# A gather's place in SBUF: eleven dead rows join the places, and the choice among them goes by expected release

## The chip, the core and the metric

The kernel runs on one core of a Trainium2 chip. The metric is the device time of one execution in microseconds (us); the time of a kernel is the median of its runs.

## What is computed

One layer of an encoder trunk over 512 tokens of width 1024, all in fp32. The first part (adaLN, a combined projection, eight heads of neighbourhood attention and four of differential attention, output projection, post-LN) takes roughly the first 315 us of the span, with its last pieces spread over what follows. The change concerns the second part, PEER retrieval, for each chunk of 128 tokens:

```python
qc = (xc @ w_query).reshape(PEER_CHUNK, PEER_HEADS, 2, PEER_DKEY // 2)
...
expert = jnp.take_along_axis(cand_i, best_j, axis=-1)     # 16 experts per token and head, 8 heads
g = jax.nn.softmax(best_s, axis=-1)
u_e = expert_down[expert]                                 # one row of 1024 floats per expert
act = jax.nn.gelu(jnp.einsum('chkd,cd->chk', u_e, xc), approximate=False)
v_e = expert_up[expert]
return jnp.einsum('chk,chkd->cd', (g * act).astype(xc.dtype), v_e)
```

With 4 chunks, 8 heads and 16 experts this is 512 sets. A set is one expert of one head for 128 tokens: it needs 128 rows of `expert_down` and 128 rows of `expert_up`, each of 4 KB, each set of rows 512 KB.

## The kernel before, in words

Tokens lie on the 128 partitions. The sets are numbered `at` = 0 to 511 in the order of `HEAD_AT`; one step through this order is called a slot below. Each set has two gathers, an indirect DMA each, of 128 rows of 4 KB into a **place**: 128 partitions by 1024 floats of SBUF.

- A **down** gather is read by VectorE at L1528: one fused product and sum with the tokens, `dots[:, at]`, then `dot_done` goes up by one. Four dots make a quarter: ScalarE takes the GELU (L993), VectorE multiplies by the gate (L1483, `weigh`), ScalarE builds four diagonal matrices `diag[:, j]` (L1163). There are 16 diagonals; that of set `at` may be built once `up_done` has reached `at - 15`.
- An **up** gather is read by TensorE at L939: two matmuls `diag[:, j]` times the place, added into a PSUM pair; each appears in the trace as two instructions, so four for a set. Then `up_done` goes up by one.

TensorE also works off `STEPS`, pieces of the remaining projections, one or more behind each up: `query` (L753), `key_scores` (L787), `ln2_row` (L735), transposes (L761). ScalarE empties their banks at L1032 at a fixed point of its own order, six slots after the group's end (`EVAC_AFTER`), and waits there for `pe_group`, which TensorE raises at the end of each group. The query groups of the later tiles lie in slots 178 to 209, 222 to 289 and 326 to 357.

GpSimd issues the gathers (L681) in the fixed order `GATHERS`: down 0, down 1, ..., and from down 7 on each down is followed by the up that lies 7 slots back, so downs and ups alternate. Before each gather stands one wait, `wait_for_place`: the place's last holder must have been read (`dot_done` or `up_done`). Which place a gather gets is fixed when the program is built. `place_for` gives the first 8 gathers places 0 to 7; a place that becomes free later is taken the first time the count of downs reaches its slot; otherwise the gather takes the place whose last holder was issued longest ago. So with k places in use each one returns k gathers later, be its holder a down or an up.

Places come in as memory dies: 8 from the start, 12 from slot 61, 16 from slot 269, 20 from slot 305 (`LATE_PLACES`, each a weight slot of four rows, released by a query group and opened `PLACE_SETS` = 16 slots later). VectorE's own order around the places: `add_mix` of the last output tile at slot 90 (`ADD_AT`), LayerNorm steps at slots 168 to 175 (`LN_FROM`), `residual(0)` and `residual(1)` after heads 12 and 16, a copy of the tokens into PSUM before every fourth head (`u_copied`).

## Time and profile before

| | us |
|---|---|
| median of 3 runs | 1824.02 |
| lowest and highest | 1817.2, 1826.44 |
| profiled execution, its own time | 1825.07 |
| its span | 1823.3 |
| first gather issued | 316.6 |
| last gather issued | 1796.4 |

The profiled execution is one of the same kind as the timed ones; 1.8 us lie around its span. The hardware profiler gives each instruction of each engine with its start and duration, each DMA packet, and the clock granted to TensorE. A wait is named by what ended it. "remote" stands there where the semaphore's update arrived and no instruction of this core that ends shortly before it can be found as its sender; "issue" where nothing of the kind ended it. The gather of one place is 0.5 MB; the share of a DMA window is the mean busy share of 16 DMA engines, GB/s what all queues moved together.

### The profile page before, as it was taken

How to read it: one execution, taken by the hardware profiler on the slowest of the kernel's cores; microseconds unless marked ns; L12 is line 12 of the kernel's file. 1: busy time of each engine (PE TensorE's matmuls, PEld its weight loads, DVE VectorE, ACT ScalarE, POOL GpSimd, SP SyncE). 2: the span in 40 equal slices, each digit the busy share in tenths (PEclk: the TensorE clock that was granted, in tenths of full speed). 3: DMA queues.
4: the chain of work that ended last, by engine and by line, in shares of the span. 5: the costliest groups of instructions: out<-in, count | busy, mean ns of one | idle time of the engine just before them, and what ended most of it. 6: DMA issues, size and time to landing. Idle time of an engine off the chain costs nothing.

```text
span 1823.3 us, 14455 instructions
## 1 busy us (share of the span) xinstructions
PE 1473.1 (81%) x4072; PEld 684.6 (38%) x4072; DVE 1116.8 (61%) x2733; ACT 438.7 (24%) x1119; POOL 983.7 (54%) x1054
## 2 busy tenths in 40 slices
PE   6999988888988897766987988876787776776775
PEld 4444557534433553222432333422343322222222
DVE  5550367776666766676565667656455674577644
ACT  3111345322221322122222222212122121122111
POOL 1000000666666666666566666666676666667663
PEclk9999999999999999998899999999898999899999
DMA  9965402999999999999899999999999999999996
GB/s 308 380 236 112 162 4 46 338 366 356 371 355 392 407 373 366 368 366 364 310 359 409 378 366 376 373 358 373 376 360 357 374 361 383 372 348 374 374 378 244
DMA packets 190617, 604.97 MB, mean 332 GB/s; under 512 B 30897, under 2 KB 31305, under 8 KB 190379
## 3 DMA queue, kind: packets, MB, share of 16 engines
q0 software_dynamic: 147456, 536.94, 77.6%
q1 hardware_dynamic: 42027, 64.30, 10.5%
q10 hardware_dynamic: 1056, 2.82, 0.5%
q8 instruction: 34, 0.56, 0.1%
q14 instruction: 44, 0.36, 0.1%
HBM read 600.64 MB, written 3.34 MB: 331 GB/s over the span
## 4 chain that ended last, share of the span: by engine, by line
PE 34%; POOL 19%; issue 14%; DMA 13%; DVE 11%; another core or an unknown queue 6%; ACT 1%; SPq 1%; DVEq 0%; POOLq 0%; ACTq 0%
PE pair L939 17%; POOL big L681 14%; PE pair L691 9%; POOL region_v L681 5%; DMA big<-in_expert_up,expert_idx 5%; DMA region_v<-in_expert_up,expert_idx 3%; DVE big L1528 3%; PE pair L753 3%; DMA big<-in_expert_down,expert_idx 2%; DMA region_v<-in_expert_down,expert_idx 2%; PE pair L779 1%; DVE region_v L1528 1%; PE pair L718 1%; SPq L519 1%
## 5 line engine op out<-in xcount | busy, mean ns | idle before, releaser
L939 PE MATMUL pair<-big 128*128 128x512 f32 x1460 | 728.7, 625 | 196.7 <-DMA big<-in_expert_up,expert_idx 93.3
L1528 DVE CUSTOM_DVE_ANT_0 big<-big,pair 128x1024 f32<-128x1024 f32 x363 | 441.2, 1219 | 267.0 <-DMA big<-in_expert_down,expert_idx 176.6
L939 PEld LDWEIGHTS pair<-big 128*128 128x128 f32 x1460 | 267.2, 196 | 576.2 <-issue 550.7
L681 POOL DMA_INDIRECT big<-in_expert_up,expert_idx x365 | 346.2, 949 | 247.7 <-remote 106.8
L681 POOL DMA_INDIRECT big<-in_expert_down,expert_idx x363 | 346.4, 954 | 123.6 <-issue 101.7
L939 PE MATMUL pair<-region_v,big 128*128 128x512 f32 x588 | 296.1, 625 | 78.9 <-DMA region_v<-in_expert_up,expert_idx 35.9
L1528 DVE CUSTOM_DVE_ANT_0 region_v<-region_v,pair 128x1024 f32<-128x1024 f32 x149 | 181.6, 1219 | 109.9 <-DMA region_v<-in_expert_down,expert_idx 75.2
L1163 ACT ACTIVATE big<-ident,big 128x128 f32<-128x128 f32 x512 | 163.5, 390 | 354.6 <-issue 185.4
L939 PEld LDWEIGHTS pair<-region_v,big 128*128 128x128 f32 x588 | 106.5, 196 | 228.2 <-issue 216.7
L681 POOL DMA_INDIRECT region_v<-in_expert_up,expert_idx x147 | 139.3, 947 | 95.4 <-issue 36.4
L681 POOL DMA_INDIRECT region_v<-in_expert_down,expert_idx x149 | 140.6, 944 | 52.1 <-issue 42.1
L993 ACT ACTIVATE big<-big 128x4 f32<-128x4 f32 x128 | 26.2, 205 | 588.1 <-issue 351.8
L691 PE MATMUL pair<-big 128*128 128x512 f32 (+1 forms) x368 | 151.0, 566 | 0.0
L753 PE MATMUL pair<-big 128*128 128x256 f32 (+1 forms) x640 | 144.3, 343 | 5.8 <-ACT big L1032 3.2
L753 PEld LDWEIGHTS pair<-big 128*128 128x128 f32 x640 | 105.8, 193 | 95.9 <-issue 90.8
L634 POOL TENSOR_SCALAR small<-x_sums 128x4 f32<-128x4 f32 x4 | 0.8, 197 | 257.0 <-ACT big L1043 257.0
L691 PEld LDWEIGHTS pair<-big 128*128 128x128 f32 x368 | 69.1, 192 | 79.9 <-issue 79.6
L1032 ACT ACTIVATE big<-pair 128x512 f32<-128x512 f32 (+2 forms) x74 | 32.9, 454 | 194.8 <-remote 158.0
L779 PE MATMUL pair<-big 128*128 128x512 f32 x128 | 63.4, 594 | 2.5 <-issue 1.6
L1483 DVE SCALAR_TENSOR_TENSOR big<-big 128x4 f32<-128x4 f32 x128 | 28.2, 220 | 48.0 <-ACT big L993 32.2
L1442 DVE CUSTOM_DVE_ANT_1 big<-pair,big 128x256 f32<-128x256 f32 x32 | 12.2, 419 | 60.1 <-PE pair L798 60.0
L993 ACT ACT_TABLE_LOAD x38 | 48.8, 1283 | 0.7
(156 smaller groups left out, 1078.1 us busy)
## 6 DMA issues: line engine op xcount, KB each, us to landing
big<-in_w_ada SPq DMA_DIRECT2D x8, 2048.0 KB, 22.3
big<-in_w_in SPq DMA_DIRECT2D x5, 2048.0 KB, 13.1
big<-in_w_ada SPq DMA_DIRECT2D x16, 512.0 KB, 11.9
big<-in_w_query SPq DMA_DIRECT2D x4, 2048.0 KB
big<-in_expert_up,expert_idx POOLq DMA_INDIRECT x365
big<-in_expert_down,expert_idx POOLq DMA_INDIRECT x363
big<-in_w_out SPq DMA_DIRECT2D x2, 2048.0 KB
big<-na_scr SPq DMA_DIRECT2D x24, 128.0 KB, 4.1
```

What stands on the lines that cost most here:

```text
L519: sp.dma_start(ada_rows[:, k, i, :].rearrange("p (a n) -> p a n", a=2), src[:, :, i, :])\
L681: nc.gpsimd.indirect_dma_start(places[place], None, (expert_down if kind == "down" else expert_up)[0], bass.IndirectOffsetOnAxis(expert_id ...
L691: last = nc.tensor.matmul(ps, a, b, start=(i == 0), stop=(i == len(pairs) - 1))
L718: last = nc.tensor.matmul(bank[b], h_t[:, k, b * P:(b + 1) * P], w_slot[ADA_FIRST][:, k, :], start=(k == 0), stop=(k == KB - 1))
L753: return nc.tensor.matmul(ps[:, 0:n * P], w_slot[query_slot(c, first)][:, k, b * P:(b + 1) * P], src, start=(k == 0), stop=(k == KB - 1))
L779: return nc.tensor.matmul(ps[:, :], src, w_slot[OUT_SLOT[s]][:, k, :], start=(k == 0), stop=(k == KB - 1))
L939: last = nc.tensor.matmul(pair[t % 2][:, s * HALF:(s + 1) * HALF], diag[:, j, :], places[place][:, s * HALF:(s + 1) * HALF], start=(h == 0 ...
L993: nc.scalar.activation(acts[:, head % 2, lo:lo + QUARTER], at_head(dots, head)[:, lo:lo + QUARTER], ACT.Gelu).then_inc(gelu_done, 1)
L1032: nc.scalar.activation(dst, ps, ACT.Copy).then_inc(act_evac, 1)
L1163: nc.scalar.activation(diag[:, j, :], ident[:, :], ACT.Copy, scale=weights[:, head % 2, j:j + 1]).then_inc(diag_done, 1)
L1483: v.scalar_tensor_tensor(out=weights[:, k, lo:lo + QUARTER], in0=gate_exps[:, k, lo:lo + QUARTER], scalar=gate_sum[:, k:k + 1], in1=acts[: ...
L1528: v.tensor_tensor_reduce(out=places[place], in0=places[place], in1=u_cur[:, :], scale=1.0, scalar=0.0, op0=ALU.mult, op1=ALU.add, accum_ou ...
```

## The change

Eleven rows of 4 KB that are dead by a given slot become places 20 to 30: a row of `mods` from slot 102, the `mix_t` region from 104, `u_sb` rows 0, 1 and 2 from slots 142, 206 and 398, the two `ln1_rows` from 188, `x_sb` rows 0 and 1 from 222 and 286, the two halves of `u_t` from 382. Each place's first gather waits for what made the row dead (`first_use`). With more than 12 places in use, an up counts as released `5 * (k - 12) // 4` gathers later than its issue order says (k places in use), so the planner takes a down's place before an up's.

```diff
+EVEN_PLACES, UP_HELD_MORE = 12, 5
+EXTRA_PLACES = [("gate", 102), ("mix", 104), ("u", 142), ("ln1_g", 188), ("ln1_b", 188), ("u", 206), ("x", 222), ("x", 286),
+                ("u_t", 382), ("u_t", 382), ("u", 398)]
...
-ALL_PLACES = PLACES + 4 * len(LATE_PLACES)
+SLOT_PLACES = PLACES + 4 * len(LATE_PLACES)
+ALL_PLACES = SLOT_PLACES + len(EXTRA_PLACES)
...
+OPEN_FROM = [0] * PLACES + [RELEASED_AT[RELEASED_BY[p]] + PLACE_SETS for p in range(PLACES, SLOT_PLACES)] \
+    + [slot for _, slot in EXTRA_PLACES]
...
+def held_until(p):
+
+    last = _held[p][-1]
+    return _order[last] + (UP_HELD_MORE * max(0, sum(map(bool, _held)) - EVEN_PLACES) // 4 if last[0] == "up" else 0)
...
-        if not _held[p] and downs >= RELEASED_AT[RELEASED_BY[p]] + PLACE_SETS:
+        if not _held[p] and downs >= OPEN_FROM[p]:
             return p
-    return min((p for p in range(ALL_PLACES) if _held[p]), key=lambda p: _order[_held[p][-1]])
+    return min((p for p in range(ALL_PLACES) if _held[p]), key=held_until)
...
+        places += [mods[:, 0, :], mix_t.rearrange("p k s -> p (k s)"), u_sb[:, 0, :], ln1_rows[:, 0, :], ln1_rows[:, 1, :],
+                   u_sb[:, 1, :], x_sb[:, 0, :], x_sb[:, 1, :], u_t_rows[:, 0, :], u_t_rows[:, 1, :], u_sb[:, 2, :]]
...
+            def first_use(place):
+
+                extra = place - SLOT_PLACES
+                if PLACES <= place < SLOT_PLACES:
+                    pool.wait_ge(pe_group, INDEX[RELEASED_BY[place]] + 1)
+                elif extra == 0:
+                    pool.wait_ge(dve_evac, EVAC[INDEX[("out", (TILES - 1, 1))]][1])
+                elif extra == 1:
+                    pool.wait_ge(pe_group, INDEX[("out", (TILES - 1, 1))] + 1)
+                elif extra == 2:
+                    pool.wait_ge(u_copied, 3)
+                elif extra in (3, 4):
+                    pool.wait_ge(u_ready, TILES)
+                elif extra == 5:
+                    pool.wait_ge(u_copied, 4)
+                elif extra in (6, 7):
+                    pool.wait_ge(var2_ready, extra - 5)
+                elif extra in (8, 9):
+                    pool.wait_ge(pe_group, INDEX[("query", (3, 3, 2, 2))] + 1)
+                elif extra == 10:
+                    pool.wait_ge(u_copied, 7)
+
             def wait_for_place(gather):
 
                 before = LAST_USE[gather]
                 if before is None:
-                    if PLACE_OF[gather] >= PLACES:
-                        pool.wait_ge(pe_group, INDEX[RELEASED_BY[PLACE_OF[gather]]] + 1)
+                    first_use(PLACE_OF[gather])
                     return
```

The gathers, their order, their number and what reads them stay as they are.

## Rows read from the trace of the kernel before

**Rows 1.** The page: busy time of the engines, and DMA in 40 slices.

```profile
PE 1473.1 (81%) x4072; PEld 684.6 (38%) x4072; DVE 1116.8 (61%) x2733; ACT 438.7 (24%) x1119; POOL 983.7 (54%) x1054
...
DMA  9965402999999999999899999999999999999996
GB/s 308 380 236 112 162 4 46 338 366 356 371 355 392 407 373 366 368 366 364 310 359 409 378 366 376 373 358 373 376 360 357 374 361 383 372 348 374 374 378 244
```

**Rows 2.** Windows by stage: engines' busy us, TensorE clock, DMA share, GB/s.

```profile
345.00:490.00 145.00, 129.31 (x405) 63.49 (x404) 102.12 (x246) 38.14 (x97) 95.77 (x101) 0.99 0.96 356
...
725.00:853.00 128.00, 90.29 (x195) 33.03 (x196) 87.08 (x214) 30.59 (x75) 85.46 (x91) 0.99 0.97 368
...
853.00:881.00 28.00, 20.79 (x33) 8.00 (x32) 11.62 (x22) 9.20 (x20) 12.24 (x14) 0.63 0.75 266
881.00:1097.00 216.00, 181.61 (x468) 82.23 (x466) 140.71 (x351) 45.99 (x123) 141.88 (x151) 0.98 0.99 376
1097.00:1205.00 108.00, 89.86 (x222) 41.14 (x223) 70.12 (x166) 26.30 (x65) 71.48 (x77) 0.97 0.98 372
1205.00:1362.00 157.00, 118.96 (x270) 50.56 (x269) 96.20 (x249) 31.26 (x85) 104.23 (x110) 0.95 0.96 367
1362.00:1795.00 433.00, 315.48 (x655) 121.69 (x653) 266.14 (x648) 88.21 (x237) 285.72 (x302) 0.94 0.97 371
```

**Rows 3.** Timeline of GpSimd at 20 places, two stops.

```profile
1216.14 0.93 POOL L681 DMA_INDIRECT big<-in_expert_down,expert_idx  x1 [0.30 <-issue]
1221.85 0.94 POOL L681 DMA_INDIRECT big<-in_expert_up,expert_idx  x1 [4.77 <-remote]
...
1253.38 0.94 POOL L681 DMA_INDIRECT big<-in_expert_down,expert_idx  x1 [0.30 <-issue]
1258.92 0.94 POOL L681 DMA_INDIRECT big<-in_expert_up,expert_idx  x1 [4.59 <-remote]
```

**Rows 4.** Timeline of TensorE: the matmuls of up 294 and of up 299.

```profile
1199.00 1.95 PE L939 MATMUL pair<-big 128*128 128x512 f32 x4 [1.15 <-DMA big<-in_expert_up,expert_idx]
...
1211.78 1.95 PE L939 MATMUL pair<-big 128*128 128x512 f32 x4 [0.61 <-issue]
```

**Rows 5.** Timeline of GpSimd at 12 places, two stops.

```profile
945.23 0.94 POOL L681 DMA_INDIRECT big<-in_expert_up,expert_idx  x1 [3.62 <-remote]
...
968.37 0.94 POOL L681 DMA_INDIRECT big<-in_expert_up,expert_idx  x1 [2.15 <-remote]
```

**Rows 6.** Windows between two stops and around one (last column GB/s).

```profile
930.00:941.00 11.00, 9.72 (x26) 4.40 (x25) 7.40 (x26) 4.26 (x8) 8.26 (x10) 1.00 1.02 410
941.00:959.00 18.00, 12.74 (x33) 5.60 (x33) 14.28 (x35) 3.23 (x11) 11.23 (x12) 1.00 0.95 344
1237.00:1254.00 17.00, 12.71 (x27) 4.37 (x26) 11.37 (x27) 5.84 (x14) 12.80 (x14) 1.00 1.03 412
1254.00:1273.00 19.00, 11.89 (x25) 4.06 (x24) 12.81 (x36) 1.69 (x6) 11.06 (x13) 1.00 0.89 325
```

**Rows 7.** Waits of GpSimd, 725 to 1795 us: total, times, longest.

```profile
POOL big L681 <- remote: 92.7, 33, 4.8
POOL region_v L681 <- remote: 20.7, 11, 3.9
POOL big L681 <- PE pair L939: 29.2, 25, 5.2
```

**Rows 8.** Timeline of GpSimd, 853 to 881 us: two waits for TensorE.

```profile
868.85 0.94 POOL L681 DMA_INDIRECT region_v<-in_expert_up,expert_idx  x1 [3.45 <-PE pair L939]
...
876.27 0.94 POOL L681 DMA_INDIRECT big<-in_expert_up,expert_idx  x1 [5.24 <-PE pair L939]
```

**Rows 9.** Waits of ScalarE, 725 to 1362 us: total, times, longest.

```profile
ACT big L1032 <- remote: 102.4, 16, 12.0
```

**Rows 10.** Timeline at 1399 us: ScalarE, GpSimd and TensorE after one stop.

```profile
1399.54 0.38 ACT L1032 ACTIVATE big<-pair 128x256 f32<-128x256 f32 x1 [16.62 <-remote]
1399.65 0.94 POOL L681 DMA_INDIRECT big<-in_expert_up,expert_idx  x1 [3.87 <-remote]
...
1400.07 2.05 PE L787 MATMUL pair<-keys_t,big 128*128 128x128 f32 x8 [10.04 <-issue]
```

More of the change, by code:

```diff
@@ L353, in build @@
         v_beside = w_flat[T5_SLOT][:, 3072:4096].rearrange("p (i d) -> p i d", i=2)
+        u_sb = region_h[:, :].rearrange("p (t d) -> p t d", t=TILES)
         places = [w_flat[T5_SLOT][:, i * D:(i + 1) * D] for i in (3, 0, 1, 2)]
@@ L357, in build @@
         places += [w_flat[slot][:, i * D:(i + 1) * D] for slot, _ in LATE_PLACES for i in range(4)]
+        u_t_rows = region_qw[:, 4096:6144].rearrange("p (i d) -> p i d", i=2)
+        places += [mods[:, 0, :], mix_t.rearrange("p k s -> p (k s)"), u_sb[:, 0, :], ln1_rows[:, 0, :], ln1_rows[:, 1, :],
+                   u_sb[:, 1, :], x_sb[:, 0, :], x_sb[:, 1, :], u_t_rows[:, 0, :], u_t_rows[:, 1, :], u_sb[:, 2, :]]
         na_place_sb = mods[0:T5_BUCKETS, 0:2, :].rearrange("p t (e m) -> p (t e) m", m=2 * P)
@@ L360, in build @@
         v_sb = region_v
-        u_sb = region_h[:, :].rearrange("p (t d) -> p t d", t=TILES)
         x_norm = region_v
```

## The prediction, made before the changed kernel was run

> **What bounds the kernel now.** I read the page first, the windows by stage second, the waits and the timeline of GpSimd third, and TensorE's and ScalarE's timelines last. The reader is to see in the page that no engine is full, while DMA stands at nine tenths from the first gather to the last [rows 1]. So the gathers set the end: 1024 of them move 537 MB. But DMA is not evenly full. Between 1237 and 1254 us it moves 412 GB/s, between 930 and 941 us 410; over whole stages it is 356 to 376 [rows 2, 6]. I take 411 as the full rate. What is missing, (1 - rate / 411) times the stage's length, is time: 19.4 us in 345 to 490, then from 725 on 13.4, 9.9, 18.4, 10.2, 16.8 and 42.1 us, in sum 110.8 us [rows 2].
>
> Where is it lost? GpSimd issues one gather every 1.24 us until it stops for 2 to 5 us, again and again: 142.6 us of such waits from 725 on, in the three largest entries [rows 7]. Each stop drains the DMA queues, and the rate is low until they have refilled. Around the stop at 941 us, 344 GB/s over 18 us makes 18 * (1 - 344/410) = 2.9 us lost; around that at 1254 us, 19 * (1 - 325/412) = 4.0 us [rows 6].
>
> What is GpSimd waiting for? At 1221.85 us the gather of up 304 starts. With 20 places its place was last held by the gather 20 earlier, that of up 294. The matmuls of up 294 ran from 1199.00 to 1200.95 [rows 4], over 20 us before GpSimd went on [rows 3]. By 1213.73 even up 299 was through [rows 4]. Either the place was free and something else stopped GpSimd, or TensorE's signal `up_done` arrives late. I take the second, for three reasons. Every long stop stands before an up. Its releaser is TensorE or "remote", an update whose sender had ended long before [rows 7]. And at 1399.5 us ScalarE, which waited 16.62 us for TensorE's `pe_group`, GpSimd (3.87 us) and then TensorE itself (10.04 us) go on within 0.6 us of each other [rows 10]. So while DMA runs full, TensorE's signals are held up, and they come in a bunch once GpSimd has stopped and the queues run down. That is read from this trace; why the chip does it I cannot see.
>
> The length of a run between stops fits. With k places GpSimd can run k/2 ups past the last known `up_done`. At 20 places the stops begin at 1217.07 and 1254.32 us, 37 us or 13 ups apart (up 304, up 317) [rows 3]; at 12 places the gathers after two stops start at 945.23 and 968.37 us, 23 us or 8 ups apart (up 208, up 216) [rows 5]. My estimate is k/2 + 2 ups on average.
>
> **The change part by part.** *The new waits.* Eleven first uses wait for the end of the row's old life. GpSimd issues down 311 at 1216.14 us [rows 3], when TensorE has just done up 299 [rows 4]: 12 slots, of which the order itself makes 7, so the readers are some 5 slots behind. Each opening slot lies at least 12 slots behind its event: 102 against `add_mix` at 90, 188 against LayerNorm's last step at 175, 222 against the residual after head 12 (slot 207), 398 against the copy before head 24 (slot 384). A slot takes 37 us / 13 = 2.85 us, so the 7 slots left over, some 20 us, cover each. The largest consumer delay seen is 16.62 us [rows 10]. I cost them at nothing; without the cover GpSimd would stand with all later gathers behind it, at 1 us per us.
>
> *The places.* A down place and an up place are no longer reused at the same distance. If a down returns after a gathers and an up after a + off, with off = 5 * (k - 12) // 4, and the two alternate, then k = a + off/2. That gives for downs and ups: 13.5 and 16.5 gathers at 15 places (from slot 142), 14 and 20 at 17 (slot 188), 15 and 23 at 19 (222), 16 and 32 at 24 (286), 18 and 38 at 28 (305), 19.5 and 42.5 at 31 (398). Before it was 12, then 16, then 20 for both. So the change gives nearly all the new room to the ups, the ones whose signals are late.
>
> *The stops.* A run of d/2 + 2 ups becomes longer. For the cost of one stop I take 2.9 us at 12 places and 4.0 at 20 [rows 6], 3.4 between, and, above 20, 4.3: a stop cannot lose more than the wait of some 4.7 us [rows 3] with the refill beside it, so the lower bound is 4.0 and the upper one is proportional growth (7 us at d = 42, with which the gain would vanish). I take 4.3 because the longest waits at 20 places are already those of a drained queue.
>
> - 725 to 853 us: runs 8 to 10 ups, cost 2.9 to 3.1: 13.4 us becomes 11.5, gain 1.9.
> - 853 to 881 us: GpSimd waits 3.45 and 5.24 us for ups that TensorE really had not done [rows 8]. With 17 places these waits go; 9.9 us lost falls to the usual 11%, 3.2: gain 6.7.
> - 881 to 1097: runs 8 to 13, cost 2.9 to 3.6: factor 0.76 on 18.4, gain 4.4.
> - 1097 to 1205: runs 10 to 17, cost 3.4 to 4.0: factor 0.69 on 10.2, gain 3.1.
> - 1205 to 1362: runs 12 to 21, cost 4.0 to 4.3: factor 0.62 on 16.8, gain 6.4.
> - 1362 to 1795: runs 12 to 23: factor 0.56 on 42.1, gain 18.5.
>
> The sum is 41.0 us.
>
> *What is late next.* ScalarE also waits for TensorE: for `up_done` at the 16-deep ring of diagonals and for `pe_group` at L1032. When GpSimd stops later, the bunch comes later, and ScalarE, then VectorE (`weigh` needs the GELU), then TensorE stand still for longer. TensorE must catch up from its slack, and each long idle also costs it clock (0.63 in 853 to 881) [rows 2]. The ring lets an up run at most 16 past the last known one, so runs of 21 to 23 are partly cut to some 16 to 19. I take 12 us off for this: a third of the 24.9 us gained behind 1205 us for the ring (8 us), and 4 us for a backlog of two ups of 1.95 us [rows 4] at the end. The net gain is 29 us: 1825.07 - 29 = 1796.1 us for the profiled execution, and 1824.02 - 29 = 1795.0 for the median, which lies 1 us below it.
>
> *Two rules of the skill.* Between stops the row shows 410 to 412 GB/s [rows 6]. The Trainium skill, "DMA: Bandwidth & Descriptors", section "Where 436 GB/s comes from", says that HBM to SBUF is bound at about 358 GB/s per core. By it the gathers already run at the limit and no choice of places could help; the trace does not agree, with 412 against 358. The stop before an up repeats all along GpSimd's row [rows 7]. The Trainium skill, "Perfetto Trace Analysis", section "Optimization Strategy", says that the same gap repeating can mean too little SBUF for the next tile. By it enough places would end all stops; the trace agrees that the stops have to do with places, but not that a longer wait for rows in use is the cause: the row had been read 20 us before.
>
> **The rivals.**
> - *Same loss at any number of places.* For it: the loss is 13% with 8 places, 8.5 to 10.5% with 12, 9.5 with 16, 9.7 to 10.7 with 20 [rows 2]. Longer runs were paid with dearer stops so far. Against it: with a drained queue the cost has a ceiling. If it holds, or if DMA has a limit of its own that the stops only follow, only the real wait of 853 to 881 us goes: 1824.0 - 6.7 = 1817.3 us.
> - *The consumers become the bound (slower).* ScalarE waited 16 times, 102.4 us in all, for `pe_group` between 725 and 1362 us [rows 9]. GpSimd's stop ends these waits today. If up distance no longer stops it, it runs until the downs do, which VectorE leaves unread once ScalarE stands. In these 637 us TensorE is busy 90.3 + 20.8 + 181.6 + 89.9 + 119.0 = 501.6 us [rows 2], so 135 are free, of which 102 go with such waits; 33 are left. The 16 waits may each grow by 33/16 = 2.1 us before TensorE bounds this stretch. Beyond that each us costs 16; the other gains (41 us) are used up from (33 + 41)/16 = 4.6 us on. At 6 us longer: 96 - 33 - 41 = 22 us slower, 1846 us. Against it: a TensorE that is behind slows the gathers through their places, DMA is then not full, and its signals come at once.
> - *All stops vanish.* The full 110.8 us: 1713 us. Against it: GpSimd's issue of 1.24 us per gather hardly leaves DMA behind, so DMA stays full, signals stay late, and each run ends sometime.
>
> **How the numbers follow.** Fewer stops 0.55 (1795; its own range 1778 to 1808), same loss 0.23 (1817), consumers bound 0.17 (1846), no stops 0.05 (1713). Leaving out "no stops" and most of the slow case, the range is 1774 to 1834 us. A measurement of this kernel can tell about 0.5%, 9 us, from no change: 1814.9 and 1833.1. Faster: all of the first and last case and a little of the second, 0.61; same: most of the second and a small part of the third, 0.22; slower 0.17.
>
> **What would show it.** Right: GpSimd's long waits before ups get rarer, some 20 from 725 us on where now some 45 stand, with waits of 4 to 5 us each; behind 1362 us the GB/s rise from 371 to about 387; the waits of 3.45 and 5.24 us are gone; ScalarE's waits at L1032 get longer. Right in places but wrong in sum: stops half as many, GB/s unchanged. Wrong: waits of GpSimd for VectorE at downs, TensorE's busy share over 90% with GpSimd waiting for it, a clock below 0.9 over long stretches. The prediction falls if the late signal is not what GpSimd waits for, or if the price of a stop grows with the length of the run before it.

## The result, and the profile after

| | before | after |
|---|---|---|
| median, us | 1825.23 (4 runs) | 1882.74 (4 runs) |
| lowest and highest | 1817.2, 1826.94 | 1865.01, 1898.14 |
| profiled execution, its span | 1825.07, 1823.3 | 1898.14, 1896.3 |
| TensorE clock over the span | 0.960 | 0.898 |
| last down gather issued | 1796 | 1850 |
| last gather issued | 1803 | 1857 |

The ratio is 1.0287, interval [1.0241, 1.0334]: 52 us slower by the ratio, 57 us between the medians of four, where 29 us faster was forecast, and outside the range. The profiled execution, 1898.14 us, is the slowest of the four and counts as a slow one, so the ratio rests on the other three. What is read from it below also stands, in kind, in the traces of two kernels close to it (e1 and e13 below, executions of 1873.7 and 1870.7 us). The 1796.4 us given for the last gather of the kernel before are those of the last down; five more ups follow it, the last at 1802.6 us.

The page of the changed kernel, the lines that answer to [rows 1]:

```profile
PE 1492.9 (79%) x4072; PEld 717.3 (38%) x4072; DVE 1108.1 (58%) x2733; ACT 437.9 (23%) x1119; POOL 989.1 (52%) x1054
...
PEclk8999999999999999997997988987787888787987
DMA  9975313999999999998999989999877999998983
GB/s 303 360 259 111 120 23 107 343 367 350 369 362 405 402 363 369 374 351 333 369 350 357 372 338 344 362 383 365 314 288 289 361 361 365 354 354 333 353 344 133
```

DMA stands at nine tenths as before, but where [rows 1] has 348 to 383 GB/s in its second half, slices of 288 and 289 stand here, and TensorE's clock falls to seven and eight tenths. Windows by stage, cut where the changed kernel issues the downs of slots 142, 188, 269, 305, 382 and 511, and behind that last down (columns as in [rows 2]):

```profile
728.00:859.00 131.00, 90.71 (x190) 33.42 (x189) 88.09 (x220) 29.86 (x73) 87.83 (x93) 0.94 0.97 370
859.00:1109.00 250.00, 200.60 (x490) 97.20 (x491) 142.86 (x358) 54.56 (x140) 154.05 (x163) 0.88 0.93 351
1109.00:1219.00 110.00, 86.77 (x225) 43.41 (x224) 72.85 (x173) 26.01 (x68) 70.03 (x72) 0.89 0.93 356
1219.00:1463.00 244.00, 173.79 (x381) 77.46 (x381) 126.93 (x333) 44.36 (x118) 146.12 (x154) 0.80 0.86 327
1463.00:1850.00 387.00, 268.71 (x533) 109.13 (x532) 230.28 (x563) 74.80 (x200) 246.99 (x261) 0.84 0.92 354
1850.00:1885.00 35.00, 25.90 (x50) 10.32 (x49) 5.58 (x13) 4.36 (x11) 5.77 (x7) 0.76 0.38 153
```

The same slots took 131.5, 241, 103, 223 and 373 us before, and 15 us lay between the last down's issue and the end of the last up, where now 34 do. So 0.3 us is won up to slot 188; then 9, 7, 21, 15 and 19 us are lost. Up to the last down the clock is 0.80 to 0.94 where [rows 2] shows 0.94 to 0.98 outside of 853 to 881 us. What GpSimd waits for, 728 to 1850 us (total, times, longest), beside [rows 7]:

```profile
POOL big L719 <- DVE big L1566: 89.3, 24, 12.0
...
POOL big L719 <- DVE expert_idx L1359: 24.4, 5, 8.5
POOL big L719 <- PE pair L977: 20.4, 16, 5.2
POOL region_v L719 <- DVE big L1566: 20.2, 9, 5.8
POOL big L719 <- remote: 19.7, 11, 4.3
POOL x_sb L719 <- DVE expert_idx L1359: 11.5, 2, 7.8
```

This is the change of kind. Before, 142.6 us of waits for TensorE or a sender unseen, and 9.8 us for VectorE, none over 0.5. Now 40.1 us of that kind in the two largest entries, and 89.3 + 20.2 + 24.4 + 11.5 = 145.4 us for VectorE: for dots (L1566), whose place a down wants, and for the experts' numbers (L1359). The waits at ups went as forecast; as much came back at downs, and a wait is now up to 12 us long and not 5.

Why is VectorE late? Here is one stop in the timeline: first GpSimd, then VectorE, then ScalarE:

```profile
1381.35 0.94 POOL L719 DMA_INDIRECT big<-in_expert_down,expert_idx  x1 [0.30 <-issue]
1386.54 0.94 POOL L719 DMA_INDIRECT big<-in_expert_up,expert_idx  x1 [4.26 <-remote]
1398.25 0.94 POOL L719 DMA_INDIRECT big<-in_expert_down,expert_idx  x1 [10.77 <-DVE big L1566]
...
1371.70 0.08 DVE L1566 DVE_READ_ACCUMULATOR2_ANT big<- 128x1 f32 x1
1395.44 0.22 DVE L1521 SCALAR_TENSOR_TENSOR big<-big 128x4 f32<-128x4 f32 x1 [23.67 <-ACT big L1031]
...
1368.06 1.28 ACT L1201 ACTIVATE big<-ident,big 128x128 f32<-128x128 f32 x4 [1.89 <-issue]
1391.89 0.38 ACT L1070 ACTIVATE big<-pair 128x256 f32<-128x256 f32 x1 [22.55 <-PE pair L791]
```

VectorE stands 23.67 us for ScalarE's GELU, ScalarE 22.55 us at an evacuation for TensorE. GpSimd goes on gathering until its downs have no place left. And TensorE? Its matmuls in the same time:

```profile
1362.42 1.88 PE L977 MATMUL pair<-big 128*128 128x512 f32 x4
...
1370.17 0.58 PE L791 MATMUL pair<-big 128*128 128x256 f32 x1 [1.48 <-issue]
1372.96 0.59 PE L791 MATMUL pair<-big 128*128 128x256 f32 x1 [2.21 <-issue]
1375.76 1.01 PE L977 MATMUL pair<-x_sb,big 128*128 128x512 f32 x1 [2.21 <-issue]
1377.88 1.01 PE L977 MATMUL pair<-x_sb,big 128*128 128x512 f32 x1 [1.10 <-issue]
1380.66 1.01 PE L977 MATMUL pair<-x_sb,big 128*128 128x512 f32 x1 [1.78 <-issue]
1383.49 1.01 PE L977 MATMUL pair<-x_sb,big 128*128 128x512 f32 x1 [1.81 <-issue]
...
1387.38 3.62 PE L977 MATMUL pair<-big 128*128 128x512 f32 x4
```

and its weight loads:

```profile
1371.57 0.29 PEld L791 LDWEIGHTS pair<-big 128*128 128x128 f32 x1 [2.52 <-issue]
1374.36 0.29 PEld L977 LDWEIGHTS pair<-x_sb,big 128*128 128x128 f32 x1 [2.51 <-issue]
1377.16 0.29 PEld L977 LDWEIGHTS pair<-x_sb,big 128*128 128x128 f32 x1 [2.51 <-issue]
```

A load at 1371.57, a matmul at 1372.96, a load at 1374.36, a matmul at 1375.76: one instruction every 1.4 us, with nothing to wait for ("issue"). Up to 1366 us an up's four matmuls took 1.88 us; from 1366 to 1387 TensorE does little more than one up in 21 us. It began 22 us after GpSimd had gone on from its last stop (1343 us) and ended when GpSimd had stopped again. The granted clock falls only at 1368.4 us, some 3 us after the stretch has begun: the clock follows the gaps here and does not start them. The windows of the full queue, the slow part, and what followed:

```profile
1354.00:1366.00 12.00, 12.00 (x33) 5.91 (x32) 8.72 (x20) 1.79 (x7) 8.90 (x10) 1.00 1.03 413
1366.00:1387.00 21.00, 6.47 (x10) 2.49 (x9) 5.78 (x11) 1.45 (x5) 12.79 (x15) 0.56 1.01 403
1387.00:1399.00 12.00, 12.00 (x27) 6.15 (x27) 3.46 (x15) 4.74 (x10) 1.23 (x2) 0.78 0.15 47
```

The second window has 10 matmuls in 21 us at a granted clock of 0.56, so mostly at the lower level of 1.2 GHz; in the third TensorE catches up while DMA moves 47 GB/s. I call this a slow stretch below, and count it so: a load or matmul of TensorE that waits for no semaphore starts 0.9 to 2.9 us after the one before it, and this happens two or more times with at most 2.9 us between them. The sums are good to some 5 us; a stricter count, without any pair closer than 0.9 us inside, gives 138 us for the changed kernel and 8 for the one before. From slot 142 on the changed kernel has 15 of them, 149 us in sum; the kernel before has 4, 20 us. The clock is at 1.2 GHz for 352 us from slot 142 on, before for 119.

### The profile page after: what moved, and what is told of

It reads as the page before. It is cut to its first block, busy times and chain, and to the rows that moved or that the text cites. A ratio compares the mean times of both kernels' runs of the same rounds, so it can differ in the third digit from the quotient of the medians.

```text
span 1896.3 us, 14455 instructions
## 1 busy us (share of the span) xinstructions
PE 1492.9 (79%) x4072; PEld 717.3 (38%) x4072; DVE 1108.1 (58%) x2733; ACT 437.9 (23%) x1119; POOL 989.1 (52%) x1054
## 4 chain that ended last, share of the span: by engine, by line
PE 32%; DVE 21%; issue 17%; another core or an unknown queue 12%; POOL 7%; DMA 7%; ACT 3%; SPq 0%; DVEq 0%; POOLq 0%; ACTq 0%
PE pair L977 16%; PE pair L729 9%; DVE big L1566 8%; POOL big L719 4%; POOL region_v L719 3%; DMA big<-in_expert_down,expert_idx 2%; DMA big<-in_expert_up,expert_idx 2%; PE pair L791 2%; PE pair L756 2%; PE pair L817 2%; DVE region_v L1566 2%; DMA region_v<-in_expert_down,expert_idx 2%; ACT big L1201 1%; PE pair L836 1%
## 5 line engine op out<-in xcount | busy, mean ns | idle before, releaser
L1566 DVE CUSTOM_DVE_ANT_0 big<-big,pair 128x1024 f32<-128x1024 f32 x360 | 433.5, 1218 | 133.3 <-DMA big<-in_expert_down,expert_idx 58.9
L977 PEld LDWEIGHTS pair<-big 128*128 128x128 f32 x1428 | 281.4, 204 | 559.6 <-issue 490.5
L719 POOL DMA_INDIRECT big<-in_expert_up,expert_idx x357 | 338.0, 947 | 184.3 <-issue 104.6
L977 PE MATMUL pair<-region_v,big 128*128 128x512 f32 x476 | 244.8, 638 | 81.4 <-issue 49.2
L791 PE MATMUL pair<-big 128*128 128x256 f32 (+1 forms) x640 | 149.9, 350 | 37.7 <-issue 35.2
L977 PEld LDWEIGHTS pair<-region_v,big 128*128 128x128 f32 x476 | 92.1, 203 | 196.9 <-issue 178.1
L1566 DVE CUSTOM_DVE_ANT_0 region_v<-region_v,pair 128x1024 f32<-128x1024 f32 x113 | 137.1, 1218 | 43.6 <-DMA region_v<-in_expert_down,expert_idx 32.3
L791 PEld LDWEIGHTS pair<-big 128*128 128x128 f32 x640 | 108.2, 197 | 133.3 <-issue 130.1
L719 POOL DMA_INDIRECT region_v<-in_expert_up,expert_idx x119 | 114.8, 965 | 63.9 <-issue 30.2
L719 POOL DMA_INDIRECT region_v<-in_expert_down,expert_idx x113 | 107.4, 950 | 63.3 <-issue 28.3
L729 PEld LDWEIGHTS pair<-big 128*128 128x128 f32 x368 | 69.1, 192 | 79.9 <-issue 79.6
L977 PE MATMUL pair<-x_sb,big 128*128 128x512 f32 x76 | 41.0, 649 | 10.7 <-issue 10.7
```

Source lines behind the costliest of these rows:

```text
L719: nc.gpsimd.indirect_dma_start(places[place], None, (expert_down if kind == "down" else expert_up)[0], bass.IndirectOffsetOnAxis(expert_id ...
L729: last = nc.tensor.matmul(ps, a, b, start=(i == 0), stop=(i == len(pairs) - 1))
L791: return nc.tensor.matmul(ps[:, 0:n * P], w_slot[query_slot(c, first)][:, k, b * P:(b + 1) * P], src, start=(k == 0), stop=(k == KB - 1))
L977: last = nc.tensor.matmul(pair[t % 2][:, s * HALF:(s + 1) * HALF], diag[:, j, :], places[place][:, s * HALF:(s + 1) * HALF], start=(h == 0 ...
L1566: v.tensor_tensor_reduce(out=places[place], in0=places[place], in1=u_cur[:, :], scale=1.0, scalar=0.0, op0=ALU.mult, op1=ALU.add, accum_ou ...
```

## The experiments

All numbers from slot 142 (some 725 us) on, except time and ratio. A stop is over 1.5 us from the end of one gather's issue to the start of the next. The ratio is to runs of the kernel before on the same chip (its medians there were 1813.2 to 1826.5 us); chips differ, so compare ratios before medians.

| kernel | median us | ratio [interval] | stops (before downs), us | slow stretches, us | at 1.2 GHz, us |
|---|---|---|---|---|---|
| before | 1825.2 | 1 | 45 (2), 147 | 20 | 119 |
| after | 1882.7 | 1.0287 [1.0241, 1.0334] | 43 (24), 199 | 149 | 352 |
| e1 rows alone | 1874.6 | 1.0263 [1.0231, 1.0296] | 36 (26), 186 | 81 | 320 |
| e2 rule alone | 1837.1 | 1.0076 [1.0048, 1.0105] | 42 (13), 150 | 69 | 221 |
| e3 after, up wait as before | 1833.5 | 1.0051 [1.0033, 1.0070] | 44 (2), 160 | 13 | 146 |
| e5 after, up wait at 6 | 1839.1 | 1.0081 [1.0058, 1.0105] | 47 (0), 169 | 0 | 68 |
| e12 after, up wait at 10 | 1832.4 | 1.0039 [1.0024, 1.0054] | 38 (1), 153 | 37 | 208 |
| e6 after, up wait at 14 | 1863.0 | 1.0229 [1.0206, 1.0251] | 47 (25), 173 | 96 | 303 |
| e8 after, ring of 32 | 1871.0 | 1.0283 [1.0247, 1.0320] | 39 (23), 154 | 188 | 336 |
| e13 after, half the signals | 1874.0 | 1.0311 [1.0250, 1.0372] | 38 (22), 170 | 119 | 315 |
| e14 before again | 1814.5 | 0.9998 [0.9981, 1.0014] | 40 (0), 137 | 13 | 142 |
| e15 before, more loads | 1845.4 | 1.0109 [1.0087, 1.0132] | 61 (1), 165 | 92 | 233 |
| e4 before, 2 empty | 1832.7 | 1.0039 [1.0023, 1.0055] | 49 (12), 116 | 13 | 92 |
| e9 before, 5 empty | 1843.1 | 1.0106 [1.0090, 1.0123] | 53 (26), 102 | 0 | 58 |
| e10 before, 8 empty | 1858.0 | 1.0197 [1.0180, 1.0214] | 6 (2), 10 | 0 | 50 |
| e7 before, 16 empty | 1906.4 | 1.0462 [1.0441, 1.0483] | 9 (8), 16 | 0 | 54 |
| e11 after, 8 empty | 1858.7 | 1.0203 [1.0186, 1.0220] | 7 (2), 12 | 0 | 43 |

### The rows, the rule, and a nearer wait

e1 keeps the eleven rows without the rule, e2 the rule without the rows:

```diff
-EVEN_PLACES, UP_HELD_MORE = 12, 5
+EVEN_PLACES, UP_HELD_MORE = 12, 0
```

> The eleven extra places alone, the up rule at zero: every place is reused at the same distance, up to 31 gathers (15.5 ups) instead of 42. Theory A (TensorE's signals arrive late while DMA is full, GpSimd's stop lets them through; an up distance beyond the 16 diagonals moves the stop from GpSimd to ScalarE, VectorE and TensorE): between before and after, 1835 to 1865 us, GpSimd's stops still mostly before ups. Theory B (the new rows themselves, or their first waits, are slow): as slow as after, 1883. Theory C (only the rule for downs, whose distance falls from 20 to 18 or 19, hurts): 1825 or less.

```diff
-EXTRA_PLACES = [("gate", 102), ("mix", 104), ("u", 142), ("ln1_g", 188), ("ln1_b", 188), ("u", 206), ("x", 222), ("x", 286),
...
+EXTRA_PLACES = []
```

> The rule alone, without the extra places: with 20 places downs return after 15 gathers and ups after 25 (12.5 ups). Theory A: slower than before by less than after, 1830 to 1860, since the up distance grows from 10 to 12.5 ups and the down distance shrinks from 10 to 7.5 downs; VectorE's waits for the GELU grow. Theory B: as before, 1825. Theory C: clearly slower, since downs fall from 20 to 15, 1850 or more.

e3 keeps both, with all 31 places, and makes each up wait as near as the kernel before did:

```diff
                 wait_for_place(gather)
+                if kind == "up" and at >= 134:
+                    pool.wait_ge(up_done, at - (6 if at < 262 else 8 if at < 298 else 10) + 1)
```

> The changed kernel with one more wait before each up gather from set 134 on: up_done must have reached what the kernel before needed at that point (6, 8 or 10 ups back). Places, rows, their first waits and both distances stay as changed. Theory A: the stops come back before ups, 20 to 37 us apart, and the time returns to that of before, 1815 to 1835, with TensorE's clock back at 0.95. Theory B and C: as after, 1883.

The rows alone cost 2.6%, the rule alone 0.8%, both 2.9%. For e1 the expectation missed: 1874.6 us lies above its 1835 to 1865, and 26 of 36 stops stand before downs, not ups. Equal distances of 31 gathers are enough for nearly the whole loss, so the rule is not what makes it. e3, with 31 places, is at 0.5%, 9.8 us above the kernel before beside it (1823.7). So the rows and their first waits cost no more than that together; what costs is that GpSimd is no longer stopped early at ups. One of e3's nine executions took 4281.8 us, for a reason not known; the median is hardly moved by it. e3's waits:

```profile
POOL big L721 <- remote: 64.2, 20, 5.6
POOL big L721 <- PE pair L979: 51.9, 31, 6.0
...
POOL region_v L721 <- DVE big L1568: 4.6, 4, 2.0
```

### The distance as a dose

The same line with one distance at all stages: `at - 6 + 1` (e5), `at - 10 + 1` (e12), `at - 14 + 1` (e6).

> The changed kernel, with all 31 places, in which each up gather from up 134 on also waits for TensorE's signal of the up 6 before it (e3_ups_waited: 6, then 8, then 10 before it, 1833.5 us). Theory A (the long run up to the downs is the cost, GpSimd must stop early and at ups): runs of about 8 ups everywhere, few or no stops before downs, ScalarE's and VectorE's long waits gone; time 1815 to 1840 us. If the price of a stop is the same at any length of run, more stops make it slower than e3: 1840 to 1860 us. Rival (the rows or the order of the places themselves cost time): 1870 us and more.

> As e5_near6, but each up gather waits for the signal of the up 14 before it, a distance between that of the kernel before (10) and the longest of the changed kernel (21). Theory A: the time lies between e3_ups_waited (1833.5 us) and the changed kernel (1882.7 us), with some 5 to 20 stops before downs from slot 142 on: 1845 to 1870 us. Rival (the diagonals' ring of 16 alone decides, any wait inside of it is harmless): within 5 us of 1833.5 us. Rival (any stop before a down costs): as the changed kernel, 1875 us and more.

> As e5_near6 (1839.1 us) and e6_far14 (1863.0 us), with the wait at the signal of the up 10 before it at every stage from up 134 on. Theory A as it stands: the price is of two kinds, stops that come oftener when the distance is short (distance 6: 47 stops, none before a down) and stops at downs with ScalarE and VectorE standing still when it is long (14: 25 of 47 before downs). Then 10 lies between or below both: 1820 to 1840 us, at most 10 stops before downs from slot 142 on. If it beats the kernel before (under 1814 us), more rows are worth something once the distance is held at 10. Rival (time grows with the distance from the shortest on): 1848 to 1855 us.

Distances 6, 10, 14 and what the changed kernel has of itself (16 and more) give ratios of 1.0081, 1.0039, 1.0229 and 1.0287; slow stretches 0, 37, 96 and 149 us; 68, 208, 303 and 352 us at 1.2 GHz. With 6 the stops are oftener (47, 169 us), with 14 half of them (25 of 47) stand before downs. The expectations held, but for the stops before downs at 14 (5 to 20 were written, 25 came). The gain over the kernel before that e12 left open did not come: even at the best distance tried, eleven more places are worth nothing. The sum of slow stretches alone doesn't set the time: e15 below has 92 us of them and loses 1.1%, e1 has 81 us and loses 2.6%. In e15 they are some 4 us long each and all stops but one stand before ups; in e1 26 of the 36 stops stand before downs, 147 us of the 186. The windows of e5 from slot 142 to the last down, then of the changed kernel:

```profile
727.00:1813.00 1086.00, 812.06 (x1836) 321.84 (x1836) 673.59 (x1648) 230.35 (x602) 701.53 (x743) 0.98 0.95 362
```

```profile
728.00:1850.00 1122.00, 820.58 (x1816) 360.63 (x1816) 661.01 (x1644) 229.61 (x598) 705.02 (x741) 0.86 0.92 349
```

### The ring of diagonals

e8 gives ScalarE a ring of 32 diagonals from slot 304 on (16 more in two rows of the last late group, so 29 places):

```diff
+        diag_more = w_flat[2][:, 2048:4096].rearrange("p (r m) -> p r m", r=TOPK)
...
-                    if at >= TOPK:
-                        act.wait_ge(up_done, at - TOPK + 1)
+                    if at >= TOPK and not MORE_FROM <= at < MORE_FROM + TOPK:
+                        act.wait_ge(up_done, at - (2 * TOPK if at >= MORE_FROM else TOPK) + 1)
```

> The changed kernel with a ring of 32 diagonals from slot 304 on (two rows of the last late group hold 16 more, so 29 places are left in place of 31). ScalarE then waits for the up 32 before and not for the up 16 before. Theory A with the ring as the main thing that holds ScalarE: faster than the changed kernel by 10 to 30 us, the gain behind slot 304. If ScalarE is held mostly by TensorE's signals of the query and score groups, which it waits for in the same order: within 5 us of 1882.7 us, with ScalarE's waits at that line as long as before.

1871.0 us is 11.7 us less than the changed kernel, but on another chip; the ratio is 1.0283 beside 1.0287, so no gain can be told. Slow stretches grew to 188 us. To let a consumer run further behind TensorE doesn't help while TensorE itself stands. Part of the loss lies at the end: from the last gather's issue to the end of the span it is 38 us in e8 and 40 in the changed kernel, where the kernel before has 21.

### Is it the full DMA queue?

e4, e9, e10 and e7 are the kernel before with 2, 5, 8 and 16 empty instructions of GpSimd ahead of each gather (from some 725 us on in the last three); e11 is the changed kernel with 8. e10's edit, the others' but for the number (e4 has no `if`):

```diff
                 wait_for_place(gather)
+                if n >= 276:
+                    for _ in range(8):
+                        nc.gpsimd.engine_nop()
```

> The kernel before with two empty instructions of GpSimd ahead of each gather, so that it issues a little slower than the 1.24 us it has now. Theory A: if the period comes to 1.29 to 1.35 us, DMA is never quite full between stops, signals come at once, the long stops become rare, and the time is 1024 times the period plus what lies outside: 1740 to 1800 us. If the signals are late for a reason other than full DMA, the period only adds: 1850 to 1900 us, with as many stops as before. If an empty instruction costs under 10 ns, no change.

> The kernel before with 16 empty instructions of GpSimd (some 0.02 us each) ahead of each gather from the 276th on, so that its period grows from 1.243 us to some 1.45 to 1.6 us. It tests whether the signals come late because the DMA queues are full. If so, with a period above the 1.276 us that a gather of 524288 bytes takes at 411 GB/s the queues are never full, the stops of 2 to 5 us before ups go, and the time is set by the period: 748 gathers at 1.45 us are 1085 us for the stretch that takes 1071 us now, so 1825 to 1870 us in all, with fewer than 10 stops. If the lateness has nothing to do with full queues, the stops stay (more than 30) and are added to the longer period: 1900 us and more.

> The kernel before with 5 empty instructions of GpSimd ahead of each gather from the 276th on (e7_paced had 16: period 1.508 us, 9 stops of over 1.5 us). The first two or three fit in the gap that is there anyway, so the period should be some 1.29 us, just above the 1.276 us that a gather takes at 411 GB/s. Theory A (signals are late because DMA runs full; with DMA not full the stops go): 748 gathers at 1.29 us and some 20 us of stops are 985 us for a stretch of 1071 us, so 1740 us; if a queue still fills up now and then, up to 1800 us. Rival (the stops' number only falls at a much slower pace): the longer period comes on top, 1835 us and more.

> As e9_pace5 with 8 empty instructions: period some 1.35 us. Theory A: 748 gathers at 1.35 us and some 16 us of stops are 1026 us in place of 1071 us, so 1780 us. Rival: 1850 us and more.

> The changed kernel (31 places) with the same 8 empty instructions ahead of each gather from the 276th on. Theory A: when the signals are in time, the order of the places no longer matters, nor do ScalarE and VectorE stand still for long: the same as e10_pace8 within 10 us. If the choice of places itself costs time (fewer places for the downs), it stays 30 us and more behind e10_pace8.

Two empty instructions fit in the 0.3 us between two issues, and the median period stayed at 1.243 us: e4 paced nothing, and is 0.4% slower. With 5, 8 and 16 it became 1.282, 1.344 and 1.508 us (medians). GpSimd's waits in e7, beside the 142.6 us of [rows 7]:

```profile
POOL big L684 <- PE pair L942: 15.2, 26, 0.7
POOL big L684 <- DVE big L1531: 14.9, 20, 1.8
```

No wait for another engine of over 1.8 us is left in e7, and there is no slow stretch. TensorE's recorded `up_done` updates show the same: before, 86 come within 0.15 us of the one ahead, in e9 3 and in e10 and e7 none. (The gaps between them say less, since some updates have no record: of some 380 there are 328 in the kernel before and 213 in e10.) The busy share of DMA hardly tells these kernels apart: 0.97 before and in e10, 0.95 in e7. The rate does: of stretches of 10 us, 35% run at 405 GB/s or more in the kernel before and 36% in the changed one, 2% in e10, 1% in e11 and none in e7. "Full" means this rate below. So bunched signals and slow stretches both go when the gathers are issued further apart. And e11 is e10 within 1 us (1858.7, 1858.0): issued so, 31 places by the new rule cost nothing, nor do they gain.

The gain I expected of pacing failed, three times: at most 1870, 1800 and 1780 us were written for 16, 5 and 8 empty instructions, and 1906.4, 1843.1 and 1858.0 came. The excess over the median period (747 periods: 150 us before, 138 in e9, 105 in e10, 31 in e7) shrank by less than the longer period added, and changed its form. In e9 GpSimd stands again and again some 1.6 us longer than its 0.34:

```profile
1306.71 0.94 POOL L684 DMA_INDIRECT big<-in_expert_down,expert_idx  x1 [0.34 <-issue]
1308.06 0.94 POOL L684 DMA_INDIRECT region_v<-in_expert_up,expert_idx  x1 [0.41 <-issue]
1310.96 0.94 POOL L684 DMA_INDIRECT region_v<-in_expert_down,expert_idx  x1 [1.96 <-issue]
```

In the raw trace an empty instruction without any wait starts at 1309.30 us there, is 11 ns long, and the next one starts at 1310.70, 1.4 us later: the same step as TensorE's. In e10 there are some 90 such delays of some 0.9 us. The mean rate is 358 GB/s (windows of e10), and that of e11 357:

```profile
726.00:1827.00 1101.00, 808.63 (x1836) 321.01 (x1836) 675.45 (x1647) 231.59 (x602) 708.41 (x742) 0.98 0.97 358
```

The kernel before has 368 GB/s over the same gathers, made of 411 and of stops. A period of 1.344 us would by itself give 524288 bytes / 1.344 us = 390 GB/s; the delays take the rest. Pacing did not beat running full and stopping. But every paced kernel also has 5 to 16 more instructions of GpSimd per gather, and the delays stand at these. No run slows the gathers without adding instructions, so what a slower issue alone would bring stays open.

### What fills up: signals or instructions?

e13 halves TensorE's `up_done` signals of the changed kernel:

```diff
-                last.then_inc(up_done, 1)
+                if at % 2:
+                    last.then_inc(up_done, 2)
```

> The changed kernel in which TensorE signals up_done once for two ups (by 2, at the odd one); waits ask for the odd one. In the trace of the changed kernel TensorE does not only signal late: after 11 to 17 signals and some 60 matmuls since GpSimd last went on, its weight loads and matmuls go one every 1.4 us though they wait for nothing (from slot 142 on 149 us in 15 stretches; in the kernel before 20 us in 4). If what fills up is a store of signals, half as many signals let the same runs end before it: the stretches at one instruction per 1.4 us shrink below 50 us and the time falls to 1835 to 1860 us. If it is something that each instruction adds to (some 60 matmuls with their loads), the stretches stay at 100 us and more and the time within 12 us of 1882.7 us.

e15 adds eight weight loads to each up of the kernel before, so 16 instructions of TensorE and not 8, with the signals as they were:

```diff
+                if at >= 134:
+                    for _ in range(8):
+                        nc.tensor.ldweights(ident[:, 0:64].bitcast(mybir.dt.bfloat16))
```

> The kernel before with 8 more weight loads (of a constant, in a 2-byte type, used by nothing) ahead of each up's matmuls from up 134 on: 16 instructions of TensorE per up in place of 8, signals and places as before. It takes the place of e14_more_instructions, whose empty instructions do not stand in its trace. If each instruction of TensorE adds to what fills up (some 60 matmuls with 60 loads in the kernels so far), TensorE falls to one instruction per 1.4 us after some 7 ups and not 12: more than 80 us of such stretches from slot 142 on, stops before downs, 1840 us and more. If it is the time that DMA has run full, or anything else that the number of instructions does not move: at most 40 us of slow stretches, and a time within 8 us of the kernel before beside it.

An earlier try with empty instructions of TensorE (e14) left none in its trace, and so was a second run of the kernel before:

> The kernel before with 8 empty instructions of TensorE more per up from up 134 on, beside the 4 weight loads and 4 matmuls of an up; signals, places and matmuls as before. If each instruction of TensorE adds to what fills up, the slow stretches begin after fewer ups: more than 80 us of them in place of 20, and 1840 us and more. If signals fill it, the time stays within 8 us of 1822 to 1826 us with at most 40 us of slow stretches. [...]

e14 gave 1814.5 beside 1813.2 us, ratio 0.9998 [0.9981, 1.0014], which shows by how much two like kernels can differ: 5 stops (45, 40), 7 us of slow stretches (20, 13), 23 us at 1.2 GHz (119, 142). e13: 119 us of slow stretches and 1.0311, no better than the changed kernel. I counted what TensorE had done between GpSimd's last going on and the start of a slow stretch: in 11 of the 15 stretches of the changed kernel 56 to 68 matmuls and 10 to 17 signals (the other four came within 9 us of a stop, after 7 matmuls or fewer), in 11 of the 13 of e13 44 to 85 matmuls and 5 to 9 signals. Half the signals, about the same number of matmuls: the signals are not what fills up. e15: slow stretches 92 us in 21 places in place of 20 us in 4, 61 stops in place of 45, 20 us slower. Its matmuls at one of them, where two ups ran at 1.8 us each just before:

```profile
1247.27 3.60 PE L942 MATMUL pair<-big 128*128 128x512 f32 x8
1251.84 1.13 PE L942 MATMUL pair<-big 128*128 128x512 f32 x2 [0.98 <-issue]
1253.24 1.31 PE L942 MATMUL pair<-big 128*128 128x512 f32 x2 [0.27 <-issue]
1260.46 2.08 PE L942 MATMUL pair<-big 128*128 128x512 f32 x2 [5.91 <-issue]
```

The same count settles more. In the median of its 21 stretches e15 had done 26 matmuls since GpSimd went on, where the 11 of the changed kernel had done 61; 11 gathers had been issued and not 21, 7 signals sent and not 14, and 13.6 us had passed and not 25.5. Only the sum of loads and matmuls is nearly the same, 101 and 122 (70 to 119 in 19 of the 21, 112 to 136 in the 11). So it isn't the time that DMA has run full, nor the gathers, signals or matmuls, but the number of TensorE's instructions, or something that goes with it; this is the onset after some 7 ups that was written down for e15. The rate in the 8 us ahead of e15's stretches was 326 to 410 GB/s and 408 to 421 within them, so the full rate need not come first. The stops before downs that I expected of e15 did not come (1 of 61).

## Why the prediction was wrong, point by point

- **What bounds the kernel.** Right: gathers at 410 to 413 GB/s between stops, and the time lost around stops. The changed kernel has 413 and 403 in its windows too.
- **The new waits cost nothing.** Not contradicted, and not shown: e3, with all rows and first waits, lies 10 us above the kernel before, and no run tells what of that is theirs.
- **The real waits at 853 to 881 us go.** Wrong. The gathers of the ups of slots 184 and 187 still wait 4.0 and 1.1 us, and that of 188 waits 5.24 us for TensorE:

```profile
886.87 0.94 POOL L719 DMA_INDIRECT big<-in_expert_up,expert_idx  x1 [5.24 <-PE pair L977]
```

  The kernel before issues that same gather at 886.5 us. What both kernels wait for in the end is up 178: with 12 places the gather of up 184 needs it, with 17 that of up 188. So the room did what was said. But TensorE ended up 178 at 876.0 us before and at 886.6 us now, having stood 8.71 and 5.37 us on the way, and that used the room up. The 6.7 us did not come, and of the 1.9 us forecast up to slot 188 came 0.3.
- **Fewer and longer runs.** Right for the ups: 19 stops before ups where 43 were, as forecast. But 24 at downs took their places, so 43 stops in all where 45 were. Behind 1362 us 387 GB/s were forecast; 354 came.
- **The price of one stop, 4.3 us at most places.** Wrong at the downs. I argued for a ceiling from a drained queue. The 19 stops before ups last 4.1 us in the mean, the 24 before downs 5.1 us and up to 12.0. The ceiling holds only if what GpSimd waits for is done by the time the queue is empty; in the wait of 10.77 us it was not, and DMA moved 47 GB/s for 12 us.
- **"I take 12 us off for this"**, in the part on what is late next: this is the step that failed. ScalarE, VectorE and TensorE standing still for longer was sized at 8 us for the ring and 4 us for a backlog at the end. The forecast gross gain of 41 us against the measured loss of 52 us by the ratio makes that term 93 us if the gains stood as forecast (114 us by the profiled executions, 1898.14 - 1825.07 = 73 us apart). At least the 6.7 us of these gains did not come, so the term is smaller by that much. The backlog alone was 19 us and not 4: 34 us from the last down's issue to the end of the last up in place of 15, because TensorE was in a slow stretch from 1838 to 1863 us and had the rest to do after it.
- **Why it was mis-sized.** I took TensorE's lateness for late news of finished work, which costs TensorE nothing. [rows 10] already had the sign: TensorE's own wait of 10.04 us with no releaser. So had the timeline of the kernel before at 1311 to 1317 us, which the prediction doesn't use, with three matmuls after gaps and nothing to wait for:

```profile
1311.73 0.59 PE L939 MATMUL pair<-big 128*128 128x512 f32 x1 [1.00 <-issue]
1314.52 1.01 PE L939 MATMUL pair<-big 128*128 128x512 f32 x1 [2.20 <-issue]
1316.63 0.58 PE L753 MATMUL pair<-big 128*128 128x256 f32 x1 [1.09 <-issue]
```

  GpSimd's early stop at an up was not only a loss to be removed: with it TensorE stayed at its speed, and without it TensorE fell to one instruction per 1.4 us after some 60 matmuls (e3, e5, e12 beside e6 and the changed kernel). The prediction had read that every long stop stands before an up; in the kernel before 43 of 45 do.
- **The rival that came true** was "the consumers become the bound", given 0.17 and 1846 us. Its threshold was a growth of 4.6 us of each of 16 waits of ScalarE. Measured up to 1379 us, the same slot: 14 waits at that line of 163.5 us in all, 11.7 us each where [rows 9] gives 6.4, so 5.3 us more, beyond the threshold. What I had held against it (a late TensorE slows the gathers through their places, so DMA is not full and signals come at once) is false: with 18 to 38 gathers of distance the gathers go on at 403 GB/s all through the slow stretch. Two of the signs named for "wrong" came: waits of GpSimd for VectorE at downs (145.4 us), and a clock below 0.9 from slot 188 on. The third, TensorE over 90% busy, did not (820.58 of 1122 us, 73%): it stood still without being full.
- **The rule on repeated gaps**: the Trainium skill, "Perfetto Trace Analysis", section "Optimization Strategy", says that the same gap repeating can mean too little SBUF for the next tile. Read as in the prediction, that enough room would end all stops, this case doesn't agree: 31 places in place of 20 gave 43 stops in place of 45, 52 us longer in sum. **The 358 GB/s**: the Trainium skill, "DMA: Bandwidth & Descriptors", section "Where 436 GB/s comes from", gets it from 716 GB/s of a memory stack divided by two cores, and the kernel runs on one. Between stops the traces still show 403 to 413. The means of 358 and 357 in e10 and e11 look like that limit, but e7, paced more slowly, has 343; no run here shows a limit at 358.

The chain, as far as runs show it: gathers 1.243 us apart without a stop (with 1.28 us and more there are no slow stretches: e9, e10, e11, e7), some 100 to 130 loads and matmuls of TensorE since the last stop (e15, and the distances 6 to 16), then one instruction per 1.4 us and the clock at 1.2 GHz; ScalarE and VectorE stand (timeline), GpSimd runs out of downs, and the queue is empty while TensorE catches up. Open: what it is that fills up. The traces hold a record of every instruction, of GpSimd's empty ones too, and each run here was recorded; no run tells the recording from a limit of the engine's own. If it is the recording, the loss would not be there without it, and this is the largest question left.

## What to carry to other kernels

A short wait that recurs is not only a loss: ask what it lets the others do. Before a wait is removed, find how long each engine runs well without it, in the stretches of the trace where it was longest, and look for instructions that are far apart with nothing to wait for. More places let GpSimd go on past the cheap stop and moved it to a dearer one, at downs that VectorE had not read. With 31 places the best of the distances tried for the ups was about 10; with 20 places, where it is 10, the rule that makes it 12.5 cost 0.8% (e2).

## What the runs showed of the hardware

- TensorE can fall to one instruction per 1.4 us with no semaphore to wait for, while DMA moves mostly 400 to 415 GB/s. It begins after 56 to 68 matmuls, each with its load, since GpSimd last went on, in 11 of 15 stretches of the changed kernel, and after a median of 26 matmuls with 75 loads in e15; in most cases it ends within 5 us of GpSimd's next stop. In the stretch shown the granted clock falls to 0.5 (1.2 GHz) some 3 us after the beginning, TensorE being busy for 6.5 of 21 us, and is back at 1.0 from 1392.3 us on, after a run of matmuls without a gap from 1387.
- Eight more weight loads of 0.1 us per up, with TensorE's matmuls busy 77% of the time (842 of 1087 us), cost 1.1% (e15).
- GpSimd has such delays too: in e9 the instruction after an empty one of 11 ns, without a wait, came 1.4 us later.
- Issuing the gathers 1.344 us apart in place of 1.243, by eight empty instructions ahead of each, removes nearly all stops over 1.5 us (6 left of 45) and yet lowers the mean rate from 368 to 358 GB/s (e10). The period alone allows 390; 105 us of delays take the rest.
